# Beginning a large shared SBUF area, and all tiles laid over it, 32 bytes further on

## The chip, the cores and the metric

The kernel runs on one core of one Trainium2 chip, in one launch. The metric is the device time of one execution in microseconds (us); the host only lays the arrays out before it. A run's time is the median of several executions.

## The reference, cut to what matters

The reference is a chain of two transformer-like blocks on 256 tokens of 1024 float32 channels. What matters here is that nearly all of it is dense products with float32 weights that are used once:

```
# first block
z  = rmsnorm(x) @ w_in                        # 1024 x (7 * 1024 + 16): conv, q, k, v, forget, gates
x += (sigmoid(g_a) * conv_branch + sigmoid(g_b) * attention_branch) @ w_out
q  = rmsnorm(x) @ peer_wq                     # 1024 x 2048, then top-16 of 128 x 128 product keys
x += sum over chosen experts of gelu(u_e . h) * gate_e * v_e     # 16384 experts
# second block
z  = rms_norm(x) @ w_in_2                     # linear recurrence, gated linear attention, memory attention
x += (sum of three gated branches @ w_branch) @ w_out_2
x += (gelu(gate) * value) @ w_down_2          # after h2 @ w_up_2 (1024 x 6144) and a 3-tap convolution
return rms_norm(x)
```

The kernel computes the experts densely: every token against all 16384 experts (the weights `in_w_u` and `in_w_ev`, 64 MB each), with gates that are zero for those not chosen.

## The kernel before, in words

**Layout.** Activations lie transposed: channels on the 128 partitions, 256 tokens along the partition. Weights arrive from memory in tiles of 128 x 1024 float32 (`raw`, two pairs), in a fixed order of chunks of two tiles (`plan_chunks`). The transfer queue of SyncE loads them in that order.

**Split products.** A float32 product is made from three products in the rounded type `F32R`. ScalarE rounds each tile `raw` into `w_hi` (L1364), GpSimd or VectorE writes the difference into `w_lo` (L462), and each activation is held the same way as a pair `*_hi`, `*_lo`. TensorE then runs hi x hi, hi x lo and lo x hi. TensorE's engine loads 128 columns of the *stationary* operand (the first one in `pe.matmul` after the output) and streams the *moving* operand (the second) past it. In the profile's names the moving operand stands first: `gemm<-h_hi,w_hi` streams `h_hi` past the weights `w_hi`.

**Stages** (L is the line in the kernel):

- `product_tile` (L679, L684): weights stationary, 256 columns of an activation moving. The activation is `h_hi`/`h_lo` for the input projections, the expert scores and the up projection, and `x_*`, `y_*`, `f_*` or `m_*` for the first chunks, the output projections, the peer queries and the second block's branches.
- `paced_product` (L700 to L731) and `first_chunk` (L742) are the same with their order broken up at the start of a stage.
- `by_token` (L813): here the activation (`h_hi`, `h_lo`, `mem_lo`) is stationary and 256 columns of the weights move.
- a tile of `product_tile` is 3 x 8 matmuls. The stretch from 284.52 to 318.60 us is 12 tiles of the peer queries, `f` (`g_parts`) moving past `w`; 61.50 to 103.49 us is 15 tiles of the first projections, `h` moving past `w`. A stretch's count in the rows below includes up to three matmuls that only touch its edges.
- `expert_values` (L982, L1010): `act_parts` is stationary and 512 columns of the weights move.
- the down projection (L1268): weights stationary, 256 columns of `f_hi`/`f_lo` moving.
- smaller products in full float32 on tiles in `big`: the forget gates (L799), attention, key scores (L932), sums over channels (L894), transposes.

Each engine runs its own program in a fixed order that is written out by hand, with semaphores between them.

**Where the tiles lie.** `sb(name, ...)` takes the next free bytes of each partition, and a tensor opened in `with ... : pass` gives its bytes back at once, so that what is allocated next lies over it. `big` (128 KB a partition) is such a one. It is carved into the stages' tiles (`q_even`, `kT`, `vtok`, `qp`, `act_peer`, `zc`, `gate`, `merged`, `uc`, `yout` and others), and the tiles `y_hi`, `y_lo`, `m_lo`, `f_hi`, `f_lo`, `x_hi`, `x_lo` lie over it.

```
raw = [[sb(f"raw{r}{v}", [P, TILE]) for v in range(2)] for r in range(RAW)]
w_hi = [sb(f"w_hi{v}", [P, TILE], F32R) for v in range(2)]
w_lo = [sb(f"w_lo{v}", [P, TILE], F32R) for v in range(2)]
...
with nc.sbuf_tensor("act_parts", [P, KD, T], F32R) as act_parts:
    pass
sb("ahead_of_h", [P, 8])
h_hi = sb("h_hi", [P, KD, T], F32R)
...
sb("behind_h", [P, 8])
```

The first bytes in a partition, as the compiled program has them, and what is left of them after division by 64 and by 256:

```
tile                     first byte  mod 64  mod 256
raw00                    16512       0       128
w_hi0                    32896       0       128
w_lo0                    41088       0       128
act_parts                57472       0       128
h_hi                     57504       32      160
h_lo                     65696       32      160
ones                     78368       32      32
small, mem_lo            81248       32      96
big, y_hi (before)       96608       32      96
f_hi (before)            121184      32      96
x_hi (before)            170336      32      96
```

The tiles' own sizes, and the steps between the eight channel groups of an activation (1024 bytes) and of the weights (512 bytes), are multiples of 256 bytes, so that each split product's operands begin with the same remainders as their tiles.

The lines of code that run on TensorE for most of the time, and the two that differ in which operand moves:

```
mm = pe.matmul(out, w[:, k, :], act_part[:, k, :], start=(n == k == 0), stop=False)            # L679
mm = pe.matmul(out, w[:, k, :], x[0][:, k, :], start=False, stop=(k == steps - 1))             # L684
mm = pe.matmul(pair(gemm[c.bank])[:, tt, :],                                                   # L813
               x[:, v * KD // 2 + k, tt * P:(tt + 1) * P], w[:, k, :], ...)
mm = pe.matmul(gemm[2 * half + tt][:, :], a[:, c.raw, v, tt * P:(tt + 1) * P],                 # L982
               w[v][:, half * (D // 2):(half + 1) * (D // 2)], ...)
mm = pe.matmul(out, w[v][:, k * P:(k + 1) * P], x[:, g * KD + k, :], ...)                      # L1268
```

Of the kernel before, what the change touches and what calls it, by code (L numbers as in the profile page):

```python
# [38 lines left out]
P = 128  # L39
# [127 lines left out]
def build(nc, t):  # L167
    plan, order = plan_chunks()
    ctx = ExitStack()
    with ctx:  # L170
        def sb(name, shape, dt=F32):
            return ctx.enter_context(nc.sbuf_tensor(name, shape, dt))
# [37 lines left out]
        mem_lo = sb("mem_lo", [P, KD, T], F32R)  # L210
        sb("small_rest", [P, 7 * T])

        with nc.sbuf_tensor("big", [P, P * T], F32) as big:
            pass

# [2549 lines left out]
```

## Time and profile before

| | |
|---|---|
| median of 3 runs | 1597.53 us (1597.45 to 1598.48) |
| span of the profiled execution | 1595.2 us (its own time outside the span is not listed) |
| TensorE (PE) busy | 1583.0 us |
| VectorE (DVE), ScalarE (ACT), GpSimd (POOL) busy | 1071.3, 884.2, 885.8 us |
| bytes moved by DMA | 277.03 MB, mean 174 GB/s |

The span runs from the first to the last recorded instruction. Busy time is the union of an engine's instructions; matmuls overlap in the pipeline, so the duration of one is longer than its share of the busy time. A group's busy time divided by its count, in a stretch that holds only that group, is the time that one matmul costs.

### The profile page before, as it was taken

How to read it: one execution, taken by the hardware profiler on the slowest of the kernel's cores; microseconds unless marked ns; L12 is line 12 of the kernel's file. 1: busy time of each engine (PE TensorE's matmuls, PEld its weight loads, DVE VectorE, ACT ScalarE, POOL GpSimd, SP SyncE). 2: the span in 40 equal slices, each digit the busy share in tenths (PEclk: the TensorE clock that was granted, in tenths of full speed). 3: DMA queues.
4: the chain of work that ended last, by engine and by line, in shares of the span. 5: the costliest groups of instructions: out<-in, count | busy, mean ns of one | idle time of the engine just before them, and what ended most of it. 6: DMA issues, size and time to landing. Idle time of an engine off the chain costs nothing.

```text
span 1595.2 us, 33476 instructions
## 1 busy us (share of the span) xinstructions
PE 1583.0 (99%) x12568; PEld 1493.5 (94%) x12568; DVE 1071.3 (67%) x1867; ACT 884.2 (55%) x1251; POOL 885.8 (56%) x413
## 2 busy tenths in 40 slices
PE   9999999999999999999999999999999999999998
PEld 8999899999999999998888888889999999999998
DVE  7998643779933777778888666776937383455521
ACT  6557766454454444444444445457676654666653
POOL 8786468868886000000000244457876689888886
PEclk9999999999999999999999999999999999999999
DMA  6565346555555555555555666666543356666653
GB/s 222 171 191 154 106 132 187 186 175 190 188 184 186 171 171 171 172 169 171 179 178 166 215 190 194 195 189 185 172 148 106 109 177 185 188 190 187 191 187 119
DMA packets 86218, 277.03 MB, mean 174 GB/s; under 512 B 11233, under 2 KB 18161, under 8 KB 86129
## 3 DMA queue, kind: packets, MB, share of 16 engines
q1 hardware_dynamic: 85712, 274.76, 54.9%
q8 instruction: 59, 0.97, 0.3%
q0 software_dynamic: 272, 1.05, 0.2%
q14 instruction: 31, 0.25, 0.1%
q10 hardware_dynamic: 144, 0.00, 0.0%
HBM read 274.73 MB, written 1.05 MB: 173 GB/s over the span
## 4 chain that ended last, share of the span: by engine, by line
PE 93%; issue 2%; DVE 2%; POOL 1%; ACT 1%; DMA 0%; SPq 0%; DVEq 0%; ACTq 0%; POOLq 0%
PE gemm L679 36%; PE gemm L982 22%; PE gemm L684 18%; PE aux L1268 4%; PE gemm L813 3%; PE aux L962 2%; POOL w_lo L462 1%; PE gemm L700 1%; PE gemm L725 1%; PE gemm L1268 1%; PE aux L932 0%; PE gemm L799 0%; ACT w_hi L1364 0%; PE gemm L706 0%; PE gemm L742 0%
## 5 line engine op out<-in xcount | busy, mean ns | idle before, releaser
L462 POOL TENSOR_TENSOR w_lo<-raw,w_hi 128x1024 fp32r<-128x1024 f32 (+1 forms) x330 | 791.7, 2407 | 294.7 <-ACT w_hi L1364 285.6
L1364 ACT ACTIVATE w_hi<-raw 128x1024 fp32r<-128x1024 f32 (+1 forms) x492 | 515.8, 1050 | 575.5 <-PE gemm L679 324.0
L679 PE MATMUL gemm<-h_lo,w_hi 128*128 128x256 f32 x2144 | 294.3, 279 | 0.0
L679 PE MATMUL gemm<-h_hi,w_hi 128*128 128x256 f32 x2096 | 293.3, 282 | 0.4 <-ACT w_hi L1364 0.3
L684 PE MATMUL gemm<-h_hi,w_lo 128*128 128x256 f32 x2096 | 288.6, 280 | 1.4 <-POOL w_lo L462 0.9
L679 PEld LDWEIGHTS gemm<-h_lo,w_hi 128*128 128x128 f32 x2144 | 268.9, 188 | 0.3 <-issue 0.2
L679 PEld LDWEIGHTS gemm<-h_hi,w_hi 128*128 128x128 f32 x2096 | 264.0, 188 | 3.3 <-issue 1.6
L462 DVE TENSOR_TENSOR w_lo<-raw,w_hi 128x1024 fp32r<-128x1024 f32 x162 | 196.6, 1222 | 104.3 <-ACT w_hi L1364 103.7
L684 PEld LDWEIGHTS gemm<-h_hi,w_lo 128*128 128x128 f32 x2096 | 262.8, 188 | 3.5 <-POOL w_lo L462 2.2
L982 PE MATMUL gemm<-w_hi,act_parts 128*128 128x512 f32 x1008 | 250.9, 391 | 0.4 <-ACT act_parts L1565 0.4
L982 PEld LDWEIGHTS gemm<-w_hi,act_parts 128*128 128x128 f32 x1008 | 188.0, 188 | 39.0 <-issue 0.5
L623 POOL DMA_DIRECT2D small<-in_memT x1 | 1.0, 1029 | 383.6 <-DVE big L2301 383.6
L982 PE MATMUL gemm<-w_lo,act_parts 128*128 128x512 f32 x504 | 134.8, 389 | 0.0
L2307 DVE TENSOR_TENSOR act_parts<-big,act_parts 128x512 fp32r<-128x512 f32 x64 | 89.2, 1393 | 48.3 <-ACT act_parts L1565 48.3
L982 PEld LDWEIGHTS gemm<-w_lo,act_parts 128*128 128x128 f32 x504 | 94.5, 188 | 19.9 <-DVE w_lo L462 0.3
L2044 DVE SCALAR_TENSOR_TENSOR aux<-big,params,aux 128x256 f32<-128x256 f32 x240 | 94.7, 491 | 0.0
L458 POOL TENSOR_TENSOR w_lo<-raw,w_hi 128x768 fp32r<-128x768 f32 x30 | 59.1, 1969 | 18.3 <-ACT w_hi L1361 17.5
L2293 DVE TENSOR_TENSOR small<-small 128x512 f16<-128x512 f16 x128 | 57.2, 489 | 0.0
L2610 DVE SCALAR_TENSOR_TENSOR big<-gemm,params,big 128x255 f32<-128x255 f32 (+1 forms) x96 | 39.7, 476 | 24.9 <-ACT big L1847 24.9
L2290 DVE TENSOR_TENSOR small<-small 128x1024 f16<-128x1024 f16 x64 | 46.0, 719 | 0.0
L2301 DVE SCALAR_TENSOR_TENSOR big<-aux,big 128x512 f32 x64 | 41.0, 683 | 0.0
L1565 ACT ACTIVATE act_parts<-big 128x512 fp32r (+1 forms) x64 | 40.1, 628 | 0.2 <-issue 0.2
(436 smaller groups left out, 2065.6 us busy)
## 6 DMA issues: line engine op xcount, KB each, us to landing
raw<-in_w_u SPq DMA_DIRECT2D x128, 512.0 KB, 3.6
raw<-in_w_ev SPq DMA_DIRECT2D x128, 512.0 KB, 3.7
raw<-in_w_up SPq DMA_DIRECT2D x48, 512.0 KB, 4.3
raw<-in_w_gate SPq DMA_DIRECT2D x24, 512.0 KB, 3.8
raw<-in_w_down SPq DMA_DIRECT2D x24, 512.0 KB, 4.0
raw<-in_w_conv_in SPq DMA_DIRECT2D x16, 512.0 KB, 4.6
raw<-in_w_peer_q SPq DMA_DIRECT2D x16, 512.0 KB, 3.5
raw<-in_w_branch SPq DMA_DIRECT2D x24, 288.0 KB, 2.9
```

Source lines behind the costliest of these rows:

```text
L458: eng.tensor_tensor(lo[:, :, 0:C96], by_k(raw[c.raw][v], C96), hi[:, :, 0:C96], ALU.subtract)
L462: eng.tensor_tensor(w_lo[v][:, 0:n], raw[c.raw][v][:, 0:n], w_hi[v][:, 0:n], ALU.subtract).then_inc(lo_ready[v], 1)
L679: mm = pe.matmul(out, w[:, k, :], act_part[:, k, :], start=(n == k == 0), stop=False)
L684: mm = pe.matmul(out, w[:, k, :], x[0][:, k, :], start=False, stop=(k == steps - 1))
L813: mm = pe.matmul(pair(gemm[c.bank])[:, tt, :], x[:, v * KD // 2 + k, tt * P:(tt + 1) * P], w[:, k, :], start=(begins and tt == k == 0), st ...
L982: mm = pe.matmul(gemm[2 * half + tt][:, :], a[:, c.raw, v, tt * P:(tt + 1) * P], w[v][:, half * (D // 2):(half + 1) * (D // 2)], start=(op ...
L1268: mm = pe.matmul(out, w[v][:, k * P:(k + 1) * P], x[:, g * KD + k, :], start=(g == k == 0 and (v == 0 or pr == 3) and w is w_hi and x is f ...
L1364: act.activation(w_hi[v][:, 0:n], raw[c.raw][v][:, 0:n], ACT.Copy).then_inc(hi_ready[v], 1)
L2044: ins = dve.scalar_tensor_tensor(acc, zc[:, k, w:w + T], tap, acc, ALU.mult, ALU.add)
L2290: dve.tensor_tensor(hot2[:, b], each(iota2, P), along(e2T[:, tokens], P), ALU.is_equal)
L2293: ins = dve.tensor_tensor(hot1[:, b, part], hot[:, b], along(gate_parts[:, part, tokens], P // 2), ALU.mult)
L2307: dve.tensor_tensor(a_lo[:, c.raw, :, :], act_peer[:, plane, :], a_hi[:, c.raw, :, :], ALU.subtract).then_inc(a_split, 1)
```

## The change

Eight floats a partition, 32 bytes, are allocated ahead of `big` and never used:

```diff
         mem_lo = sb("mem_lo", [P, KD, T], F32R)
         sb("small_rest", [P, 7 * T])
 
+        sb("ahead_of_big", [P, 8])
         with nc.sbuf_tensor("big", [P, P * T], F32) as big:
             pass
```

`big` and `y_hi` then begin at byte 96640, `f_hi` at 121216, `x_hi` at 170368: remainder 0 by 64 and 128 by 256. Nothing that is allocated ahead of them moves. Every engine's instructions, their order, their waits and their shapes are the same as before; only the addresses of operands that lie in `big` or over it are 32 bytes higher. Line numbers of the kernel behind this line are one higher.

## Rows read from the trace of the kernel before

**Rows 1.** The page: busy time, share of the span and instructions of each engine.
```profile
PE 1583.0 (99%) x12568; PEld 1493.5 (94%) x12568; DVE 1071.3 (67%) x1867; ACT 884.2 (55%) x1251; POOL 885.8 (56%) x413
```

**Rows 2.** The page: the clock granted to TensorE in 40 slices, in tenths.
```profile
PEclk9999999999999999999999999999999999999999
```

**Rows 3.** The page: the chain that ended last, share of the span by engine.
```profile
PE 93%; issue 2%; DVE 2%; POOL 1%; ACT 1%; DMA 0%; SPq 0%; DVEq 0%; ACTq 0%; POOLq 0%
```

**Rows 4.** Waits of PE, the two longest in total (waited for, times, longest us).
```profile
PE aux L790 <- POOL zeros L589: 1.3, 1, 1.3
PE gemm L684 <- POOL w_lo L462: 1.2, 4, 0.3
```

**Rows 5.** PE in five stretches (stretch, length, busy (count), clock, DMA share, GB/s).
```profile
61.50:103.49 41.99, 41.99 (x362) 1.00 0.63 198
103.49:126.20 22.71, 22.71 (x195) 1.00 0.64 187
284.52:318.60 34.08, 34.08 (x291) 1.00 0.62 199
1007.03:1066.88 59.85, 59.85 (x265) 1.00 0.63 196
1518.18:1572.13 53.95, 53.95 (x459) 1.00 0.60 187
```

**Rows 6.** The chain in order of time: pieces in these stretches (start us, us, what).
```profile
100.69 1.87 PE gemm L679 x16
103.49 22.71 PE gemm L813 x192
...
301.56 1.89 PE gemm L679 x16
303.46 0.95 PE gemm L684 x8
304.40 1.89 PE gemm L679 x16
...
321.49 7.25 PE aux L932 x64
...
328.74 1.87 PE gemm L679 x16
...
1007.03 59.85 PE gemm L982 x264
...
1518.18 53.95 PE aux L1268 x456
```

**Rows 7.** PE over the whole span, tile by tile: y_hi, y_lo, m_lo, f_hi, f_lo, x_hi, x_lo.
```profile
0.00:1595.20 1595.20, 35.24 (x256) 1.00 0.55 174
0.00:1595.20 1595.20, 17.58 (x128) 1.00 0.55 174
0.00:1595.20 1595.20, 8.71 (x64) 1.00 0.55 174
0.00:1595.20 1595.20, 109.84 (x832) 1.00 0.55 174
0.00:1595.20 1595.20, 51.19 (x368) 1.00 0.55 174
0.00:1595.20 1595.20, 56.72 (x416) 1.00 0.55 174
0.00:1595.20 1595.20, 26.40 (x192) 1.00 0.55 174
```

**Rows 8.** PE over the whole span: the tiles h_hi, h_lo, act_parts, and big.
```profile
0.00:1595.20 1595.20, 589.68 (x4512) 1.00 0.55 174
0.00:1595.20 1595.20, 334.67 (x2448) 1.00 0.55 174
0.00:1595.20 1595.20, 353.06 (x1536) 1.00 0.55 174
0.00:1595.20 1595.20, 98.96 (x650) 1.00 0.55 174
```

**Rows 9.** Line 2044 on DVE (count: duration ns min/median/max).
```profile
L2044 DVE SCALAR_TENSOR_TENSOR aux<-big,params,aux x240: 481/490/502, 27.5 to 125.6; 128x256 f32<-128x256 f32 x120
```

**Rows 10.** The chain in order of time: full float32 products of 256 columns.
```profile
54.94 3.56 PE gemm L799 x16
...
144.69 1.74 PE aux L894 x8
```

**Rows 11.** Issues of DMA that write or read big (count, KB each, us to landing).
```profile
yT<-big SPq DMA_DIRECT2D x4, 256.0 KB, 2.4
big<-in_w_mem_k SPq DMA_DIRECT2D x2, 384.0 KB, 4.0
big<-in_w_zg SPq DMA_DIRECT2D x2, 384.0 KB, 3.9
```

**Rows 12.** The chain in order of time, its end (start us, us, what).
```profile
1583.49 2.85 PE gemm L1268 x24
...
1590.88 1.20 DVE big L2673 x2
```

## The prediction

> **What bounds the kernel now.** I read the page first. TensorE is busy for 1583.0 of 1595.2 us [rows 1], at a granted clock of nine tenths or more in every slice [rows 2] and of 1.00 in the stretches used below [rows 5], which is its level of 2.4 GHz, and the chain that ended last runs through it for 93% of the span [rows 3]. TensorE hardly waits: its two largest entries are 1.3 and 1.2 us [rows 4]. So the end moves when matmuls become shorter or longer, and by little else.
>
> Then I asked what one matmul costs in steady state, since an address can act on nothing but the reading and writing of operands. A column at 2.4 GHz is 0.417 ns, so 256 columns are 106.7 ns and 512 are 213.3 ns. I divided stretches [rows 5] by the matmuls that the code issues in them (24 a tile, or the counts of the chain [rows 6]). "Distance" is the first byte of the moving operand less that of the stationary one, after whole multiples of 256 bytes are taken away:
>
> - `h` past `w`, distance +32: 41.99 us / 360 = 116.6 ns, 9.9 above its columns.
> - `f` past `w`, distance -32: 34.08 / 288 = 118.3 ns in L679 and L684, and 53.95 / 456 = 118.3 ns in L1268: 11.6 above.
> - `w` past `h` (L813), distance -32: 22.71 / 192 = 118.3 ns: 11.6 above.
> - `w` past `act_parts` (L982), distance 0, 512 columns: 59.85 / 264 = 226.7 ns: 13.4 above.
>
> The reader should see three things. Every split product has 10 to 13 ns that are not columns. Code being equal (the first two both run `product_tile`, written out), the address makes 1.7 ns of difference. And it is not the address of one operand that counts: L813 and L1268 exchange which of the two has remainder 0 by 64, and cost the same. It is the distance. The change takes the distance of all `f`, `x`, `y` and `m` products from -32 to 0, where of all split products only L982 stands today.
>
> **The change part by part.** It adds and removes no instruction, wait or transfer.
>
> *Split products with an operand over `big`.* The seven tiles' counts are 256 + 128 + 64 + 832 + 368 + 416 + 192 = 2256 matmuls [rows 7]. The 4512 + 2448 with `h` and the 1536 with `act_parts` [rows 8] keep their addresses. No row shows a product with 256 columns at distance 0. Bounds:
>
> - Above: the extra of L982 is one for each weight load, whatever number of columns streams. Then it is 13.4 ns at 256 columns too, 1.8 ns more than today's 11.6: 2256 x 1.8 ns = 4.1 us. Against the cheapest product, the `h` stretch, the step is 13.4 - 9.9 = 3.5 ns; if the move from -32 cost as much as that whole step, it would be 7.9 us.
> - Below: the extra of L982 grows with the columns. Then 256 columns have half of it, 6.7 ns, which is 4.9 ns less than today: 2256 x 4.9 ns = 11.1 us gained. In between lies the price of distance +32, 9.9 ns: 1.7 ns less, 3.8 us gained.
> - I take the first, +4.1 us. The reason is what full float32 products show. L894 streams 256 columns in 1.74 / 8 = 217.5 ns and L799 in 3.56 / 16 = 222.5 ns [rows 10], two cycles a column and so as long as one of L982, and they have only 4 and 9 ns that are not columns (starts of the groups included). So streaming for a long time is not what costs 13 ns; it comes up when both the moving operand and the next weights are read at the full rate. The next weights are 128 columns in L982 as in all others, and so the extra should be one for each load.
>
> *Full float32 products on `big`* (650 matmuls, 98.96 us [rows 8]). Where both operands lie in `big` their distance stays. The key scores, L932, go from one distance to 0: 64 matmuls, 7.25 / 64 = 113.3 ns each [rows 6]. With 1.8 ns on each it would be 0.1 us. I take zero.
>
> *VectorE, ScalarE and GpSimd on `big`.* The convolution's taps (L2044) read one tile at 31 starts, 4 bytes apart, and so pass through every remainder by 64. All 240 take 481 to 502 ns [rows 9], and VectorE stands in 2% of the chain [rows 3], 32 us, of which even 1% is 0.3 us. I take zero, with 0.3 us to either side.
>
> *Transfers.* The spare tiles (`big<-in_w_mem_k` to `big<-in_w_zg`) land in 3.9 to 4.0 us [rows 11], ahead of their use. The four output transfers of 2.4 us [rows 11] come last, behind VectorE's last products at 1590.88 us [rows 12], with no cover. Sizes and counts stay; I take zero.
> By the Trainium skill (DMA: Bandwidth & Descriptors, How a descriptor splits into AXI transactions) a descriptor that does not begin on 256 bytes also fetches what lies between the boundary below and its start, in beats of 32 bytes. For 1024 bytes of `yout` that is 35 beats at remainder 96 before and 36 at remainder 128 after; as an estimate from the page, under 0.1 us against the change. No row here shows it.
>
> *Sum.* 4.1 us on the span of 1595.2, so 1599.3. The runs' median of 1597.53 is 2.3 us above the profiled span; with the same 2.3 us the time is 1601.6. What a measurement of this kernel can tell from no change is about 0.2%, 3.2 us or 1.4 ns on each of the 2256.
>
> **Rivals.**
>
> 1. *No change.* The distance may matter only for its sign or by larger powers of two (`f` stands 224 bytes past `w` by 1024 today and 256 after, L982 at 0), and 0 may be as good as -32. For it: 1.8 ns of 226.7 is under 1%, and two prices 1.7 ns apart are thin ground. Against it: the address has an effect, and a new distance has no reason to cost just the same. The time: 1597.5.
>    By the Trainium skill (TensorE: Matmul & The Clock Gate, Step-by-step: what each phase is for) the engine has two independent read ports, and loading the next weights takes nothing from the running matmul. By that no distance would matter and the time is 1597.5. The trace disagrees in part: 118.3 against 116.6 ns for the same code.
> 2. *Faster: distance 0 is the cheap one.* Both streams begin on the same remainder and keep out of each other's way, and L982's extra comes from its columns. TensorE's share falls by 3.8 us at the price of +32, by 11.1 us at half of L982's. It decides from 1.4 ns a matmul on. For it: L982 loses 13.4 ns in 512 columns, fewer in each column than any other. Against it: its weight load is as long as theirs, and if two streams meet, equal remainders are where they do. The time: 1593.7, or 1586.4 at the full price.
> 3. *The tiles do not move as the diff says*: excluded by the addresses in the compiled program.
>
> **How the numbers follow.** Slower by over 0.2%: 0.44, the constant extra of L982 and what lies above it. No change: 0.32, which also holds smaller effects of either sign. Faster by over 0.2%: 0.24, of which I give 0.12 to the price of +32 and 0.12 to more. The predicted time is the likeliest case's, 1601.6. The range begins at 1593.5, under the price of +32, and leaves out the large gain; it ends at 1605.3, near the step of 3.5 ns (7.9 us). The likeliest case's own range is 1600.7 to 1605.3.
>
> **What would show it.** In the profile after, L1268's piece of 456 matmuls, 53.95 us before, is 54.8 us if I am right, 53.95 under the first rival, and 53.2 or 51.7 under the second. The 12 tiles of the peer queries, 34.08 us before, go with it: 34.6, 34.1, and 33.6 or 32.7. The stretches of `h`, L813 and L982 stay. The taps of L2044 stay between 481 and 502 ns. The prediction is wrong if L1268's price moves by less than 1.4 ns or falls, or if time appears in another engine's work on `big`.

## The result, and the profile after

The changed kernel takes 1601.58 us (median of 10 runs, 1601.26 to 1604.45) against 1597.58 us for the kernel before (10 runs): a ratio of 1.0026, with a 95% interval of 1.0017 to 1.0035. It is slower, by 4.0 us. The forecast was 1601.6 us. One of the ten executions of the last experiment below took 8959 us, against 1600 to 1604 for the others, and its ratio leaves it out.

The page of the kernel after, busy time by engine, beside [rows 1]:

```profile
span 1599.4 us, 33476 instructions
PE 1587.2 (99%) x12568; PEld 1497.3 (94%) x12568; DVE 1065.4 (67%) x1867; ACT 884.7 (55%) x1251; POOL 886.3 (55%) x413
```

The instructions are the same in number. TensorE's busy time and the span are both 4.2 us longer; no other engine has grown by more than 0.5 us.

The chain of the kernel after in order of time (start us, us, what), beside [rows 6]. Its code lines stand one higher than before:

```profile
103.88 22.73 PE gemm L814 x192
...
285.68 1.92 PE gemm L680 x16
287.59 0.96 PE gemm L685 x8
...
320.23 1.92 PE gemm L680 x16
323.15 7.25 PE aux L933 x64
...
1008.70 59.85 PE gemm L983 x264
...
1521.44 54.70 PE aux L1269 x456
```

What to see: the down projection, `f` past `w`, now takes 54.70 / 456 = 120.0 ns a matmul where it took 118.3. The 12 tiles of the peer queries between 285.68 and 320.23 us take 34.55 us, 120.0 ns, where they took 34.08. L814 (`w` past `h`), L983 (`w` past `act_parts`) and the key scores L933, whose full float32 operands also moved, cost what they did.

TensorE over the whole span by tile, in the order of [rows 7] (y_hi, y_lo, m_lo, f_hi, f_lo, x_hi, x_lo), and then `h_hi` and `act_parts`, beside [rows 8]:

```profile
0.00:1599.40 1599.40, 35.60 (x256) 1.00 0.54 173
0.00:1599.40 1599.40, 17.80 (x128) 1.00 0.54 173
0.00:1599.40 1599.40, 8.82 (x64) 1.00 0.54 173
0.00:1599.40 1599.40, 111.15 (x832) 1.00 0.54 173
0.00:1599.40 1599.40, 51.81 (x368) 1.00 0.54 173
0.00:1599.40 1599.40, 57.23 (x416) 1.00 0.54 173
0.00:1599.40 1599.40, 26.68 (x192) 1.00 0.54 173
...
0.00:1599.40 1599.40, 589.81 (x4512) 1.00 0.54 173
...
0.00:1599.40 1599.40, 353.07 (x1536) 1.00 0.54 173
```

The seven tiles' sum is 309.09 us against 305.68 before: 3.4 us of the 4.2 stand in just the 2256 matmuls whose operands moved. `h_hi` and `act_parts` stand still, within 0.13 us. Most of the rest is filler at the start: the first weights took 5.21 us to arrive, 4.84 before, and the filler products on `zeros` that TensorE runs in that time grew from 4.42 to 4.99 us. The granted clock is 1.00 in both.

### The profile page after: what moved, and what is told of

It is laid out like the page before. It is cut to its first block, busy times and chain, and to the rows that moved or that the text cites. A ratio compares the mean times of both kernels' runs of the same rounds, so it can differ in the third digit from the quotient of the medians.

```text
span 1599.4 us, 33476 instructions
## 1 busy us (share of the span) xinstructions
PE 1587.2 (99%) x12568; PEld 1497.3 (94%) x12568; DVE 1065.4 (67%) x1867; ACT 884.7 (55%) x1251; POOL 886.3 (55%) x413
## 4 chain that ended last, share of the span: by engine, by line
PE 93%; POOL 2%; issue 2%; DVE 2%; ACT 1%; DMA 0%; SPq 0%; DVEq 0%; ACTq 0%; POOLq 0%
PE gemm L680 36%; PE gemm L983 22%; PE gemm L685 18%; PE aux L1269 4%; PE gemm L814 3%; PE aux L963 2%; POOL w_lo L463 1%; PE gemm L701 1%; PE gemm L726 1%; PE gemm L1269 1%; ACT w_hi L1365 0%; PE aux L933 0%; PE gemm L800 0%; PE gemm L707 0%; PE gemm L743 0%
## 5 line engine op out<-in xcount | busy, mean ns | idle before, releaser
L983 PE MATMUL gemm<-w_hi,act_parts 128*128 128x512 f32 x1008 | 251.0, 391 | 0.4 <-ACT act_parts L1566 0.4
L983 PEld LDWEIGHTS gemm<-w_hi,act_parts 128*128 128x128 f32 x1008 | 188.0, 188 | 39.0 <-issue 0.5
L983 PE MATMUL gemm<-w_lo,act_parts 128*128 128x512 f32 x504 | 134.8, 389 | 0.0
L983 PEld LDWEIGHTS gemm<-w_lo,act_parts 128*128 128x128 f32 x504 | 94.5, 188 | 19.9 <-DVE w_lo L463 0.3
L459 POOL TENSOR_TENSOR w_lo<-raw,w_hi 128x768 fp32r<-128x768 f32 x30 | 58.9, 1964 | 18.6 <-ACT w_hi L1362 17.7
```

Of the source, the lines that this page charges most:

```text
L459: eng.tensor_tensor(lo[:, :, 0:C96], by_k(raw[c.raw][v], C96), hi[:, :, 0:C96], ALU.subtract)
```

## The experiments

Two readings of the result had to be told apart: that the *distance* between the moving and the stationary operand, signed and by 256 bytes, sets the price of a split product, or that something coarser does (whether the two agree by 64 bytes; the absolute place; the area over `big` itself). Then the forecast's reason for the price at distance 0, one extra for each weight load, was tested by itself.

All four kernels of the first group differ from the kernel before only in where tiles begin. Each ratio is against runs of the kernel before on the same chip as the experiment; chips differ, so its median is given beside it. For this group it is 1599.38 us.

### 16 floats ahead of big: distance +32

```diff
-        sb("ahead_of_big", [P, 8])
+        sb("ahead_of_big", [P, 16])
```

> 16 floats instead of 8 ahead of big: the products on f, x, y and m have distance +32 (moving less stationary, by 256), as h has. Distance theory: a split product costs 116.7 ns at +32, 118.3 at -32 and 120.0 at 0; so they fall to 116.7 ns, the down projection's 456 matmuls take 53.2 us, and the time is 1597.6 - 2256 x 1.67 ns = 1593.8 us. Parity theory (only whether the two remainders by 64 are equal counts, and what sets h apart from f is something else): they return to 118.3 ns and the time is 1597.6 us.

Measured: 1596.62 us, ratio to the kernel before 0.9979 (0.9970 to 0.9989): 2.8 us less, where 3.8 were expected. The chain of this kernel:

```profile
9.04 7.05 PE gemm L743 x44
...
106.11 22.71 PE gemm L814 x192
...
1008.50 59.85 PE gemm L983 x264
...
1519.02 53.20 PE aux L1269 x456
```

53.20 / 456 = 116.7 ns, the price that `h` has at +32. The distance theory holds, and parity falls: the remainders by 64 are as unequal as before the change, and yet each matmul costs 1.7 ns less. This kernel beats both. Its profiled span, 1595.0 us, hides this: L814 began 2.6 us later than in the kernel before. One half of that is the first transfer, 6.16 us against 4.84. The other half is the first chunk's 44 products, 7.05 us against 5.75: behind the longer wait they ran at a mean granted clock of 0.76, between TensorE's levels of 1.2 and 2.4 GHz, where the kernel before had 1.00. Neither belongs to the addresses: the same +32 in a later run (half of each load, below) had a granted clock of 1.00 there and reached L814 at 104.32 us, 0.8 us later than before.

### 24 floats ahead of big: distance +64

```diff
-        sb("ahead_of_big", [P, 8])
+        sb("ahead_of_big", [P, 24])
```

> 24 floats ahead of big: distance +64, both remainders by 64 equal to 0. Parity theory: 120.0 ns as in the change, 1601.6 us. Distance theory: a value of its own that nothing has shown yet; if the price has a period of 64 bytes it is 120.0 ns as well, which the pair +32 and -32 speaks against; I expect 116.7 to 118.3 ns, 1593.8 to 1597.6 us.

Measured: 1596.85 us, ratio 0.9984 (0.9975 to 0.9994). The down projection takes 53.71 us, 117.8 ns. Parity falls a second time: the remainders by 64 are equal and the price isn't 120.0. But the price is not one number here. In the same kernel the products of `x` and `m` in the second block run faster behind one break (the piece of 8 that takes 1.10 us). The chain:

```profile
1365.79 1.88 PE gemm L680 x16
1367.67 1.10 PE gemm L685 x8
1368.77 1.81 PE gemm L680 x16
1370.59 0.91 PE gemm L685 x8
...
1517.88 53.71 PE aux L1269 x456
```

1.88 / 16 = 117.5 ns before the break and 1.81 / 16 = 113.1 ns behind it, for the same code and distance. Pieces of 16 are good to 0.3 ns only; a whole tile behind the break, (1371.49 - 1368.77) / 24, gives 113.3 ns, and the dear price is the 117.8 ns of the down projection within that.

### The 32 bytes ahead of h moved behind it: distance 0 for h

```diff
-        sb("ahead_of_h", [P, 8])
         h_hi = sb("h_hi", [P, KD, T], F32R)
...
-        sb("behind_h", [P, 8])
+        sb("behind_h", [P, 16])
```

> The kernel before with the 32 bytes ahead of h moved behind it, so that h_hi and h_lo have distance 0 to the weights and all else stays. Distance and parity theory: the products with h moving go from 116.7 to 120.0 ns (some 6480 of them, 21.6 us), L813's from 118.3 to 120.0 (0.6 us), f, x, y and m stay at 118.3: about 1619.8 us. Rival, that the tiles over big are a case of their own (the change's effect is bound to the place in memory): h stays at 116.7 ns and the time is 1597.6 us.

Measured: 1617.11 us, ratio 1.0106 (1.0090 to 1.0121): 17.7 us more than the kernel before on this chip, where 22.2 were expected. The profiled span is 1615.8 us, 20.6 more than in the profile of the kernel before. The chain (lines here are one lower than before):

```profile
106.89 23.04 PE gemm L812 x192
...
341.59 1.92 PE gemm L678 x16
343.51 0.96 PE gemm L683 x8
...
1538.81 53.96 PE aux L1267 x456
```

`h` past `w` costs 1.92 / 16 = 120.0 ns, `w` past `h` 23.04 / 192 = 120.0 ns, and `f`, unmoved, 118.3 ns as ever. So the effect is not bound to the area over `big`; it follows the distance there and here.

### Both operands at remainder 32, distance 0

```diff
+        sb("ahead_of_w", [P, 8])
         w_hi = [sb(f"w_hi{v}", [P, TILE], F32R) for v in range(2)]
...
+        sb("ahead_of_big", [P, 8])
         with nc.sbuf_tensor("big", [P, P * T], F32) as big:
```

> 32 bytes ahead of w_hi, which moves all tiles behind raw, and 32 bytes more ahead of big: the products on f, x, y and m have distance 0, but both operands begin at remainder 32 by 64; those on h keep their distance of +32. Distance and parity theory: as in the change, 120.0 ns for f and 116.7 ns for h, 1601.6 us. Rival, an absolute rule (a product is dear when both operands begin on a multiple of 64): f at 118.3 ns or less, 1597.6 us or less.

Measured: 1602.76 us, ratio 1.0020 (1.0010 to 1.0029). The chain:

```profile
103.91 22.71 PE gemm L815 x192
...
1521.54 54.72 PE aux L1270 x456
```

The down projection takes 120.0 ns, as in the change, and L815 118.3 ns. No absolute rule: two operands that both begin 32 bytes off cost the same as two that begin on a multiple of 64.

### The change with half of each weight load

```diff
-                            mm = pe.matmul(out, w[v][:, k * P:(k + 1) * P], x[:, g * KD + k, :],
+                            mm = pe.matmul(out[0:64], w[v][:, k * P:k * P + 64], x[:, g * KD + k, :],
```

> The change, with the down projection (L1269) loading and computing only the first 64 of each 128 weight columns, so that half of its output is left out; its moving operand keeps its 256 columns and the distance is 0. If the extra of a split product is a price of the weight load that meets the stream (13.3 ns for 128 columns, 120.0 ns in all), half the load costs half: 113.3 ns, and 456 matmuls take 51.7 us. Rival, a fixed price of each matmul or of its 256 streamed columns: 120.0 ns and 54.7 us as in the change.

This kernel leaves out half of the down projection's output. Measured in the one execution timed, 1597.99 us; down projection:

```profile
1521.78 51.69 PE aux L1269 x456
```

51.69 / 456 = 113.4 ns: 6.7 ns above the 106.7 of its columns, where the whole load has 13.3. Half the load, half the extra. The rows also bear out the 106.7 ns: at distance 0, 512 columns cost 226.7 ns and 256 cost 120.0, so 256 more columns are 106.7 ns and the extra doesn't grow with them. At distance 0 the extra is a price of the load, or of what the edit halves with it: `out[0:64]` also writes to half of the partitions, and no run parts the two at distance 0.

### act_parts moved, so that its moving weights stand at +32

L982 with its stationary operand 224 bytes further on, on the kernel with 16 floats ahead of `big`:

```diff
-        with nc.sbuf_tensor("act_parts", [P, KD, T], F32R) as act_parts:
+        with nc.sbuf_tensor("ahead_of_act", [P, 56], F32), nc.sbuf_tensor("act_parts", [P, KD, T], F32R) as act_parts:
...
+        sb("between_h", [P, 256])
         with nc.sbuf_tensor("mem_sq", [P, KD, T], F32) as mem_sq:
```

> The kernel of 16 floats ahead of big, with act_parts 224 bytes further on (and 1024 bytes between h_hi and h_lo to make room), so that L982's weights stand at +32 past act_parts and not at 0. Distance theory: L982 goes from 226.7 to 213.3 + 10.0 = 223.3 ns, 1536 x 3.3 ns = 5.1 us less than with 16 floats alone, 8.9 us less than the kernel before. Rival, that what lies above the 512 columns comes from their number: L982 stays at 226.7 ns and the time is that of 16 floats alone.

The 256 floats of `between_h` keep `act_parts` clear of `h_lo` and move what lies behind them by 1024 bytes, a multiple of 256. Measured: 1606.92 us, ratio 1.0039 (1.0026 to 1.0053) against a median of 1599.79. L982 (here L984) became slower:

```profile
1018.26 61.60 PE gemm L984 x264
```

61.60 / 264 = 233.3 ns: 20.0 ns above the 213.3 of 512 columns, twice the 10.0 ns of 256 columns at the same distance. My expectation of 223.3 ns was wrong by 10 ns, and the time rose by 7.1 us where a fall of 8.9 was expected.

### Half of each weight load at distance +32

The edit of L1268 above, on the kernel with 16 floats ahead of `big`.

> 16 floats ahead of big (distance +32), and the down projection (L1269) loads and computes only the first 64 of each 128 weight columns, so half of its output is left out. At distance 0 half the load gave half the extra. If at +32 the extra (10.0 ns) is also a price of the load, 106.7 + 5.0 = 111.7 ns and 456 matmuls take 50.9 us. If at +32 it comes with the streamed columns, as the doubling of L982's extra to 20 ns at 512 columns suggests, it stays at 116.7 ns, 53.2 us.

Measured, down projection:

```profile
1518.48 53.20 PE aux L1269 x456
```

116.7 ns with half the load as with the whole. At +32 the extra of 10.0 ns is no price of the load's length, and halving the output's partitions changes nothing there either.

### act_parts moved, so that its moving weights stand at -32

```diff
-        with nc.sbuf_tensor("act_parts", [P, KD, T], F32R) as act_parts:
+        with nc.sbuf_tensor("ahead_of_act", [P, 8], F32), nc.sbuf_tensor("act_parts", [P, KD, T], F32R) as act_parts:
```

> 16 floats ahead of big, and act_parts 32 bytes further on, so that in L982 the moving w stands at -32 past act_parts. If the extra is one for each load at every distance, it is 11.6 ns, 225.0 ns in all, 1.7 ns less than at 0. If away from 0 it grows with the streamed columns, it is 23.3 ns, 236.7 ns in all, 1536 x 10.0 = 15.3 us more.

Measured in the one execution timed, 1604.82 us:

```profile
1014.47 61.59 PE gemm L983 x264
```

Again 233.3 ns. That is 20.0 ns, neither the 11.6 of one theory nor the 23.3 of the other. At +32 and -32 the extra grows with the streamed columns, though at -32 not in full proportion (11.6 ns for 256). For L982 distance 0 is the cheap one of the three, at 13.3 ns, and for 256 columns it is the dear one. Only this line of code streams 512 columns, so that the columns and not something else of this line are what counts is argued, not shown.

### Other distances

32 and 40 floats ahead of `big`, each a kernel by itself:

```diff
-        sb("ahead_of_big", [P, 8])
+        sb("ahead_of_big", [P, 32])
...
-        sb("ahead_of_big", [P, 8])
+        sb("ahead_of_big", [P, 40])
```

> 32 floats ahead of big: distance +96. If the price repeats every 128 bytes it is that of -32, 118.3 ns (53.9 us for the 456 of the down projection); if it repeats only every 256 bytes or more, a value of its own: I expect 116 to 118 ns.

> 40 floats ahead of big: distance +128. If the price repeats every 128 bytes it is that of 0, 120.0 ns (54.7 us for the 456 of the down projection); if only every 256 bytes or more, something below 118 ns.

```profile
1524.94 54.72 PE aux L1269 x456
```

```profile
240.61 1.92 PE gemm L680 x16
...
1522.85 54.12 PE aux L1269 x456
```

One execution of each was timed, 1604.99 and 1601.81 us. The down projection of the first, at +96, costs 54.72 / 456 = 120.0 ns, that of the second, at +128, 54.12 / 456 = 118.7 ns. But the second too has stretches at another price: the products of `x` from 240.61 us on take 1.92 / 16 = 120.0 ns. The price at +96 is not that of -32 (118.3 ns), which speaks against a period of 128 bytes, and my guess for it was 2 ns too low. The second says less, as it shows the price of 0 as well. What speaks for 256 is that pairs of places 256 or more apart agree: 120.0 ns for `h` at 0 and `f` at 256 by 1024 bytes, 116.7 ns for `h` at 32 and `f` at 288.

Then the kernel before with other amounts around `h`, 48 and 16 floats in one run and 16 and 24 in the last:

```diff
-        sb("ahead_of_h", [P, 8])
+        sb("ahead_of_h", [P, 48])
...
-        sb("behind_h", [P, 8])
+        sb("behind_h", [P, 16])
```

> 48 floats ahead of h and 16 behind it in place of 8 and 8, nothing ahead of big: h stands at +192 (the same as -64) to w, L813's w at +64 to h, and the tiles over big at +160 (the same as -96). Two values of their own: with 120.0, 116.7, 117.8, 120.0, 118.7 ns at 0, +32, +64, +96, +128 and 118.3 at -32, I expect 116 to 120 ns for both. L813 at +64 should take 117.8 ns as the down projection did there, if the rule is one of distance by 256.

> 16 floats ahead of h and 24 behind it, so that h, mem_lo and the tiles over big all stand at +64 to w, and L813's w at -64 to h. At 64 bytes' distance two prices were seen for the same code and addresses, 113.4 ns and 117.8 ns, each kept for whole stages until TensorE waits. If a stage keeps the state with which it begins, each stretch shows one of the two and nothing between; the time is then between 1587 us (all cheap: 9200 matmuls x 3.3 ns less than at +32, for about a third of them) and 1602 us (all dear). Rival, that only the distance counts: one price in all stages.

Measured, the first: 1599.53 us in the one execution timed (1600.05 for the kernel before), and two prices for the same code at -64. The chain of that kernel around one change of price, and L813 with `w` at +64:

```profile
102.34 21.77 PE gemm L813 x192
...
445.17 1.88 PE gemm L679 x16
447.06 0.94 PE gemm L684 x8
448.00 1.88 PE gemm L679 x16
449.88 0.00 issue
449.89 1.20 PE gemm L684 x8
451.08 1.81 PE gemm L679 x16
452.90 0.91 PE gemm L684 x8
...
464.69 0.66 PE aux L950 x6
465.34 1.89 PE gemm L679 x16
```

The expert loop runs at 1.88 / 16 = 117.5 ns (117.9 by a whole tile, (448.00 - 445.17) / 24) until its run is broken at 449.88 us, then at 113.1 ns (113.3 by a tile) until six transposes come between, and then at 118 ns again. L813 takes 21.77 / 192 = 113.4 ns, so my 117.8 ns for it was wrong. The tiles over `big`, at -96, have more than one price too:

```profile
203.92 1.92 PE gemm L679 x16
...
301.66 1.90 PE gemm L679 x16
...
1521.04 53.51 PE aux L1268 x456
```

That is 120.0 ns in one output projection's tile, 118.7 in the peer queries and 53.51 / 456 = 117.3 ns in the down projection. In the kernels with distances of 0, +32 and -32 each of these three pieces costs what the down projection does, to 0.3 ns.

The last kernel, all at +64 or -64: 1601.39 us, ratio 1.0020 (1.0010 to 1.0030) against a median of 1598.44. Its chain has the cheap price at the start and in a few later pieces:

```profile
51.67 1.81 PE gemm L679 x16
...
54.39 3.56 PE gemm L799 x16
57.95 2.08 PE gemm L679 x16
...
60.97 1.88 PE gemm L679 x16
...
103.36 22.61 PE gemm L813 x192
...
1099.94 10.00 PE gemm L813 x88
...
1522.01 53.71 PE aux L1268 x456
```

113.1 ns up to the forget gates' 16 full float32 products (L799) and 117.5 ns behind them, the same two prices as above. The first stretch of L813 takes 117.8 ns, against 113.4 in the run with 48 floats, and a later one of this kernel 10.00 us / 88 = 113.6 ns. So at 64 bytes a stretch of code keeps the price with which it comes out of a break, as expected; which of the two it gets isn't told by the distance, and nothing here shows what decides it. Most stages came out dear, and the time lies at the upper end of what I had given.

## Why the prediction was right, point by point

- *What bounds the kernel.* TensorE, and the end moved with its matmuls: 4.2 us more busy time, 4.2 us more span.
- *The address counts, as a distance.* Read from three prices of the trace before (116.6, 118.3 and 118.3 ns). The runs with `h` at 0, both at remainder 32, and `big` at +32 and +64 confirmed it for 0, +32 and -32 and excluded the other readings. As "the distance sets one price" it is too strong: at +64, -64, -96 and +128 the same distance had two prices or more in one kernel.
- *The term of the sum.* 2256 matmuls x 1.8 ns = 4.1 us was forecast; the rows after show 120.0 - 118.3 = 1.7 ns, 3.8 us by the count and 3.4 us in the tiles' busy time. Of the remaining 0.8 us of TensorE's busy time 0.6 stand in the filler products on `zeros` (4.99 against 4.42 us), with the first transfer 0.37 us longer; L814 began 0.4 us later. Nothing here ties that to the change: in the chains of the experiments' kernels the same transfer took 4.98 to 6.82 us. So the mechanism and the size of the term were right, to 0.3 us, and that 1601.6 was met to the tenth is luck: the term came out a little smaller and the start a little longer.
- *The reason for taking 13.4 ns and not 6.7.* I held that the extra is one for each load, whatever streams past. At distance 0 that is what happens: half the load halves it, and 256 and 512 columns have the same 13.3 ns. As a general rule it is wrong: at +32 the load's length does not matter and the extra doubles with the columns. The full float32 rows that led to it also bear less than was put on them: L799, with 9 ns, loads just 16 columns at a time, and only L894, with 4 ns, loads 128 as the split products do. The forecast needed it at distance 0 only, and there it held. Had L982 stood at another distance, the same argument would have misled; my expectation of 223.3 ns for it at +32 fell for just this.
- *The full float32 products and the transfers.* L933 took 7.25 us before and after. The four output transfers landed in 2.5 us where they took 2.4. Zero was right, to 0.1 us.
- *VectorE.* I said that the taps would stay between 481 and 502 ns. After the change they took 483 to 519, so that sign failed, but in the run with `h` at 0, where their tile has the address of before, they took 471 to 486. So they differ as much between runs at one address as with the change, and they did not set the end: VectorE's busy time fell by 5.9 us while the span grew. (L2044 has 30 of the 31 starts; the first tap is another line.)
- *The rivals.* No change (0.32) and faster (0.24) did not come; three prices were thin ground to choose on, as the 0.44 says. The faster one had a true core: the extra of 6.7 ns that it set as its full price does occur with a whole weight load, in the 113.1 to 113.4 ns at 64 bytes' distance, but not at distance 0.
- *The two read ports.* By the Trainium skill (TensorE: Matmul & The Clock Gate, Step-by-step: what each phase is for) loading the next weights takes nothing from the running matmul. The runs differ: with the same instructions the extra went from 10.0 to 13.3 ns by moving one operand by 32 bytes, and at distance 0 it halved when the weight load (and with it the output) was halved. At +32 halving the load changed nothing, as that sentence would have it.

## What to carry to other kernels

When TensorE is full and its operands stream at one column a cycle, compute from the trace what each matmul costs above its columns, stage by stage, and set it beside the distance of the operands' first bytes; a step of 32 bytes in an allocation was worth 0.3% here for 2256 matmuls and 1.1% for some 6900. Do not carry a price from one shape to another: distance 0 was among the dearest with 256 columns and the cheapest of three with 512. Do not take it from one stretch alone either: at four of the eight distances tried stretches of one kernel differed. And move operands on purpose rather than as a side effect of a tile put in ahead of them.

## What the runs showed of the hardware that I had not expected

With split products of 128 loaded and 256 streamed columns, at a granted clock of 1.00, one matmul cost, by the distance of the moving from the stationary operand by 256 bytes: 120.0 ns at 0, 116.7 at +32, 118.3 at -32, 117.8 or 113.4 at +64 and at -64, 120.0 at +96, 118.7 or 120.0 at +128, and 117.3, 118.7 or 120.0 at -96. With 512 streamed columns: 226.7 ns at 0, 233.3 at +32 and at -32. Full float32 products did not show it (L933 113.3 ns at +32 and at 0).

The start times of the single matmuls in the down projection differ in kind as well. At distance 0 each starts 120 ns behind the one before. At -32 the steps run from 115 to 123 ns and repeat, with 118.3 as their mean, and at +32 from 113 to 120, with 116.7.

At 64 bytes' distance the same code has two prices 4.4 ns apart, and in the pieces shown it changes between them only at breaks. A kernel that kept the cheap one throughout its 9200 products with 256 columns would, as an estimate, save some 30 us against +32 (9200 x 3.3 ns). Whether a break of the right length could bring that about was not tried. Why the price depends on the distance at all stays open too: two streams that meet in the memory fit the behaviour at distance 0, where the load sets the price, and do not by themselves explain +32, where it doesn't.
